# The opening of a two-block model on one core: order of the first loads, one projection alone, rotary angles and turned roots elsewhere, one sum of squares later

## The chip, the cores and the metric

One core of a Trainium2 chip runs the whole program in one launch. The metric is the device time of an execution in microseconds (us). The kernel before takes 2652.35 us (median of three runs, 2652.09 to 2652.76).

## The reference, cut to what matters

Everything is float32. 512 tokens of width 1024 go through a first block of two layers and then a second block (attention, short convolution, a mixture of 32 experts). The change lies in the first block. One layer of it, in short:

```python
y = rms_norm(h, mix_norm[i])                       # root of the mean square over 1024
proj = y @ w_in[i]
x_lru, g_lru, q, k, v, g_ret, u_sgu, v_sgu, g_sgu = jnp.split(proj, split_points, axis=-1)
lru_out = rg_lru(causal_depthwise_conv(x_lru, ...), w_a, b_a, w_x, b_x, lru_lambda[i])   # recurrence
ret_out = retention(q, k, v, positions, ret_norm[i])   # q, k turned by cos/sin(positions * inv)
sgu_out = spatial_gating(u_sgu, v_sgu, ...)
mixed = concat(lru_out * silu(g_lru), ret_out * silu(g_ret), sgu_out * silu(g_sgu))
h = h + mixed @ w_out[i]
z = rms_norm(h, ple_norm[i])
h = h + sigmoid(z @ w_ple_gate[i]) * (p[i] @ w_ple_proj[i])
```

Inside `rg_lru`: `log_a = -8 r softplus(-lambda)`, `a = exp(log_a)`, `u = sqrt(1 - a^2) (i x)` and a scan over the tokens.

## The kernel before, in words

Features lie on the partitions and the 512 tokens on the columns: `hT` is x transposed, eight tiles of 128 x 512. A program of its own runs on each engine, written out in order; semaphores are the only ties between them.

**Weights** come as pieces of 128 x 1024 (512 KB), in the order of `LAYER`: `xl0 xl1 xl2 gl0 xl3 xl4 xl5 gl1..gl5`, then `lru0.*`, `v0.0..v0.3`, `gr0 gr1`, `lru1.*`, `v1.*`, `gr2..gr5`, and q, k, vs, gs, u, wo, g. SyncE (SP) loads them into five raw places (`A_RAW`); a place is free when the piece in it has been split, or, for the unsplit `lru` pieces, used. ScalarE (ACT) makes the high part (a rounded copy, L1786, L1805) and GpSimd (POOL) the low part (L2316), into four places (`A_SPLIT`). `ahead(name)` on ACT splits every piece up to four behind `name`, each as soon as the last use of the place is past. So piece `v0.3` is split by `ahead("gl5")`.

**A product** takes three matmuls per tile of the reduction (high x high, high x low, low x high), so a projection (`project`, 128 outputs) has 24 matmuls of 512 columns. The rows (`ys`) are x times the gain, as a high part (ACT, `gained_high`, L1779) and a low part (VectorE, DVE, `gained_low`, L2037). The norm's factor is not in them: results are multiplied by 1/root (`rn`) when they are read. `side_by_side` runs three projections through the row tiles together, so that it starts with the first tile; it wants all three pieces split first.

**The root**: ACT squares the tiles (L1768), DVE adds them (L2044), TensorE (PE) sums over the partitions with a matrix of ones (`norm_sum`), ACT takes the root (L1773), DVE inverts it (`norm_inverse`, L2053). In layer 0 the sum stands at tile 7 of `side_by_side`, in layer 1 at tile 3, and there it waits for `sq_added`, the whole sum over eight tiles.

**PSUM** has eight banks, in two rings of four: V (gates and others) and A. A group in a ring waits until the one four before it has been read. `gl0..gl5` are V's first six, so `gl4` waits for `gl0`, and `gl5` for `gl1`. DVE scales a gate (L2076), ACT takes its tanh (L1820), and DVE multiplies (`silu2`, L2082), which frees the bank.

**DVE's order after the inverse**: `conv(0..2)`, small work, `scale_gate("gl0")`, `conv(3..5)` with small work between (L2095, L2097, L2100), then in layer 0 `prep_angles` (20 instructions with L1994 first and L2011 last, cosine and sine angles together), then the gates `gl1..gl5`, then the recurrence: decay rates (L2124), three ratios with a reciprocal each (L2130 to L2134), three times the scan (L2140 to L2147), the gates `gr0`, `gr1`.

**ACT's order there**: gates and `ahead`s; `prep_sin` (layer 0, L1744, L1745); tanh of `r` and `i` (L1842, L1844); `ahead("gl5")`; three times Exp and Tanh for DVE's ratios (L1850, L1851); the copy of the turned root `rT` (L1853), whose drain frees its bank (L1854), for which the matmuls of `v0.3` wait; `ahead("v0.3")`; the copies of `v0` (L1858); three square roots (L1862); `gr0`, `gr1`. The second half of the recurrence (g = 1) starts on ACT when `lru_done` has come to 3, and PE's group `r5` waits for ACT's tanh of `r3`.

**Loads at the start**: SP issues piece 0, x0, piece 1, x1, piece 2, x2..x7, pieces 3 and 4. ACT issues `par`, `par2` and the positions (one row spread over 128 partitions), all three on one semaphore, and ACT and DVE wait for all three (48) before their first work.

Of the kernel before, what the change touches and what calls it, by code (L numbers as in the profile page):

```python
# [209 lines left out]
def build(nc, io):  # L210
    ctx = ExitStack()
    with ctx:
# [166 lines left out]
        A = Groups(nc, ctx, "a", [4, 5, 6, 7], a_order, pre=1)  # L379
# [16 lines left out]
        par_in = sem("parameters_in")  # L396
# [1057 lines left out]
        @block.sync  # L1454
        def _(sp):
            for n in range(A_RAW):
                if n < 3:
                    sp.dma_start(pieces[:, n, :], io["pieces"][n]).then_inc(p_in[n], 16)
                for kt in range(n, n + 1) if n < 2 else range(2, DK) if n == 2 else ():
                    sp.dma_start(hT[:, kt, :], io["xT"][kt * P:(kt + 1) * P, :]).then_inc(x_in[kt], 16)  # L1460
                if n >= 3:
                    sp.dma_start(pieces[:, n, :], io["pieces"][n]).then_inc(p_in[n], 16)
# [21 lines left out]
        def _(pe):  # L1484
# [13 lines left out]
            def norm_sum(layer, g, n):  # L1498

                pe.wait_ge(sq_added, n)  # L1500
                pe.wait_ge(A.free, A.reusable(layer, g) if layer >= 0 else 1)
                mm(ps[:, A.bank(g), :], ones[:], sq_sum, True, True).then_inc(A.full, 1)

            for layer in range(L):
# [22 lines left out]
                def side_by_side(pool, names, first, sums):  # L1527


                    ws = [wps[:, L_AT[g] % A_SPLIT].rearrange("p c (k n) -> p c k n", k=DK) for g in names]  # L1530
                    for g in names:
                        high_of(L_AT[g])
                        low_of(L_AT[g])
                        if layer == 0 and L_AT[g] == 1:
                            pe.wait_ge(first_low, 1)
                        pe.wait_ge(pool.free, pool.reusable(layer, g))
                    for k in range(DK):
                        at_ = layer * 2 * DK + first + k + 1
                        pe.wait_ge(yh_ready, at_)
                        for g, w in zip(names, ws):  # L1540
                            mm(ps[:, pool.bank(g), :], w[:, 0, k, :], ys[:, 0, k, :], k == 0, False)
                            mm(ps[:, pool.bank(g), :], w[:, 1, k, :], ys[:, 0, k, :], False, False)
                        sums(k)
                        pe.wait_ge(y_ready, at_)
                        for g, w in zip(names, ws):
                            m = mm(ps[:, pool.bank(g), :], w[:, 0, k, :], ys[:, 1, k, :], False, k == DK - 1)
                            if k == DK - 1:
                                m.then_inc(pool.full, 1)
# [178 lines left out]
        def _(act):  # L1727
            act.dma_start(par_all[:], io["par"]).then_inc(par_in, 16)
            act.dma_start(par2[:], io["par2"]).then_inc(par_in, 16)
            act.dma_start(tmp[:, 2, :].bitcast(I32), io["positions"].partition_broadcast(P)).then_inc(par_in, 16)  # L1730
            def prep_exp():
                act.wait_ge(par_in, 48)
# [3 lines left out]
            def prep_log():  # L1736
                act.wait_ge(prep_v, 2)
                nc.scalar.activation(prep_l, prep_w, ACT.Ln).then_inc(prep_a, 1)
# [3 lines left out]
            def prep_sin():  # L1742
                act.wait_ge(prep_v, 3)
                nc.scalar.activation(rcos, tmp[:, 0, :], ACT.Sin)  # L1744
                nc.scalar.activation(rsin, tmp[:, 1, :], ACT.Sin).then_inc(prep_a, 1)  # L1745
                act.drain()
# [35 lines left out]
            act.wait_ge(par_in, 48)  # L1782
            for k in range(DK):
                if k < 3:
                    act.wait_ge(*landed(0, k))
                    nc.scalar.activation(wps[:, k, 0], pieces[:, k, :], ACT.Copy).then_inc(p_high, 1)  # L1786
# [4 lines left out]
            for k in (DK - 2, DK - 1):  # L1791
                square(k, x_in[k], 16, 0, 0)
            act.wait_ge(*landed(0, 3))
            nc.scalar.activation(wps[:, 3, 0], pieces[:, 3, :], ACT.Copy).then_inc(p_high, 1)

            for layer in range(L):
# [16 lines left out]
                norm_root(A, layer - 1, "next")  # L1813
                if layer == 0:
# [19 lines left out]
                if layer == 0:  # L1834
                    prep_sin()

                for g in range(2):
# [9 lines left out]
                    ahead("gl5" if g == 0 else "gr1")  # L1847
# [15 lines left out]
                    if g == 0:  # L1863
                        ahead("gr0")
# [83 lines left out]
        def _(dve):  # L1948
            dve.sem_inc(V.free, len(V.banks))
# [4 lines left out]
            dve.wait_ge(par_in, 48)  # L1954
# [25 lines left out]
            def prep_rate():  # L1980
                dve.wait_ge(prep_a, 3)
                nc.vector.tensor_tensor(prep_c, prep_c, prep_l, ALU.add)
# [9 lines left out]
            def prep_angles():  # L1992
                posi, ang, turn, turni = tmp[:, 2, :], tmp[:, 3, :], mix[:, 6, :], mix[:, 7, :]
# [4 lines left out]
                for out, quarter in ((tmp[:, 0, :], 0.25), (tmp[:, 1, :], 0.0)):  # L1998
                    nc.vector.tensor_scalar(turni.bitcast(I32), ang, 1.0 / (2 * np.pi), quarter, ALU.mult, ALU.add)
                    dve.drain()  # L2000
                    nc.vector.tensor_copy(turn, turni.bitcast(I32))
                    dve.drain()
                    if quarter:
                        nc.vector.tensor_scalar(turn, turn, -quarter, None, ALU.add)
                        dve.drain()
                    nc.vector.scalar_tensor_tensor(out, turn, -TWO_PI[0], ang, ALU.mult, ALU.add)
                    dve.drain()
                    for part in TWO_PI[1:]:
                        nc.vector.scalar_tensor_tensor(out, turn, -part, out, ALU.mult, ALU.add)
                        dve.drain()  # L2010
                    nc.vector.tensor_scalar(out, out, 3.1415925, -3.1415925, ALU.min, ALU.max)  # L2011
                    dve.drain()
                dve.sem_inc(prep_v, 1)
# [41 lines left out]

            for k in range(DK):
                if k == 2:
                    dve.wait_ge(p_high, 2)
                    nc.vector.tensor_tensor(wps[:, 1, 1], pieces[:, 1, :], wps[:, 1, 0].bitcast(F32),
                                            ALU.subtract).then_inc(first_low, 1)  # L2060
                gained_low(k, 0, 0, "mix_norm")
                if k >= 3:
                    add_square(k - 2, 0, 0)
            for k in range(DK - 2, DK):
                add_square(k, 0, 0)

            for layer in range(L):
# [4 lines left out]
                norm_inverse(2 * layer + 1)  # L2072

# [41 lines left out]
                conv(5)  # L2115
                if layer == 0:
                    prep_angles()
                gates([f"gl{i}" for i in range(1, 6)], lambda i: 1 + i, 1)

                for g in range(2):  # L2120
# [5 lines left out]

                    for m in range(3):
# [175 lines left out]
        def _(pool):  # L2303
            def constants_in():
                for dst, name in ((ident[:], "ident"), (tri[:], "tri"), (cst[:], "cst")):
# [18 lines left out]
            for n in range(A_SPLIT):  # L2324
                if n == 1:
# [161 lines left out]
```

## Time and profile before

| what | us |
|---|---|
| median of the runs | 2652.35 |
| profiled execution | 2650.75 |
| its span, first to last instruction | 2648.9 |
| TensorE busy | 2501.9 (94%) |
| VectorE busy | 1896.0 (72%) |
| ScalarE busy | 1326.5 (50%) |
| GpSimd busy | 727.6 (27%) |
| mean granted TensorE clock | 0.974 |

The span is what the trace covers; the profiled execution's own time has 1.85 us more around it. Times in the rows are from the span's start. Layer 0 goes to about 488 us, layer 1 to about 1009 us; the second block fills the rest. A loop's matmuls overlap: one shows 389 ns, but the starts follow each other closer.

### The profile page before, as it was taken

To read this page: it belongs to the slowest core of one execution; us is meant where nothing else is said; L and a number is where in the kernel's file an instruction comes from. 1 tells how busy PE (TensorE), PEld (TensorE's weight loads), DVE (VectorE), ACT (ScalarE), POOL (GpSimd) and SP (SyncE) were. 2 spreads that over 40 slices of the span, in tenths; PEclk is the share of its full clock that TensorE was granted. 3 is DMA by queue.
4 is the path that set the end of the run, shared out by engine and by line. 5 is a ranking of instruction groups with operands and counts; after the bars stand their busy time and mean duration, and the time that the engine had idled before them with its cause. 6 is when DMAs were issued, how large, how long until landed. Compare 5 with 4: busy or idle time off the path is not lost.

```text
span 2648.9 us, 32704 instructions
## 1 busy us (share of the span) xinstructions
PE 2501.9 (94%) x11479; PEld 1987.2 (75%) x11479; DVE 1896.0 (72%) x1732; ACT 1326.5 (50%) x1224; POOL 727.6 (27%) x401
## 2 busy tenths in 40 slices
PE   7799999999999998899886999999999999999995
PEld 6577788676777875687465788888888888888884
DVE  6668541565876053276425999999999999999994
ACT  4342233424313232233423777777777777777772
POOL 4324265342424630034122212222111222111220
PEclk9899999999999999999986999999999999999998
DMA  6223232223323326523005999999999999999993
GB/s 210 87 96 88 64 120 88 72 64 112 104 71 104 96 88 224 191 64 94 3 12 207 369 371 377 366 371 370 366 372 374 366 369 370 367 371 375 368 364 104
DMA packets 104497, 572.57 MB, mean 216 GB/s; under 512 B 14193, under 2 KB 14337, under 8 KB 54353
## 3 DMA queue, kind: packets, MB, share of 16 engines
q1 hardware_dynamic: 93552, 539.27, 54.9%
q0 software_dynamic: 10432, 31.81, 4.8%
q8 instruction: 52, 0.85, 0.1%
q10 hardware_dynamic: 432, 0.40, 0.1%
q14 instruction: 29, 0.23, 0.0%
HBM read 559.37 MB, written 24.12 MB: 220 GB/s over the span
## 4 chain that ended last, share of the span: by engine, by line
PE 86%; DVE 7%; ACT 2%; DVEq 2%; issue 1%; DMA 1%; ACTq 1%; SPq 0%; POOL 0%; POOLq 0%
PE ps L1486 83%; PE ps L1167 2%; DVE scr L2100 1%; DVE y_split L2037 1%; DVEq L2047 1%; PE ps L643 0%; DVE mix L2147 0%; DVE scr L2145 0%; DMA pieces<-in_pieces 0%; DMA scr<-in_positions 0%; ACTq L1854 0%; DMA acc_rows<-rows,lst 0%; DVEq L2275 0%; DVE scr L958 0%; DVE w_split L1294 0%
## 5 line engine op out<-in xcount | busy, mean ns | idle before, releaser
L1294 DVE TENSOR_TENSOR w_split<-raw,w_split 128x2048 fp32r<-128x2048 f32 x386 | 877.5, 2288 | 54.4 <-ACT w_split L1246 43.6
L1486 PE MATMUL ps<-y_split,pieces_split 128*128 128x512 f32 x3600 | 840.0, 394 | 32.8 <-POOL pieces_split L2316 17.7
L1246 ACT ACTIVATE w_split<-raw 128x2048 fp32r<-128x2048 f32 x386 | 735.9, 1916 | 198.1 <-PE ps L1486 178.3
L1486 PEld LDWEIGHTS ps<-y_split,pieces_split 128*128 128x128 f32 x3600 | 677.9, 189 | 183.1 <-issue 40.9
L1486 PE MATMUL ps<-w_split,rows_T 128*128 128x512 f32 x3096 | 753.5, 394 | 1.9 <-DVE rows_T L1300 1.9
L1486 PEld LDWEIGHTS ps<-w_split,rows_T 128*128 128x128 f32 x3096 | 576.5, 189 | 119.8 <-DVE rows_T L1300 2.5
L2316 POOL TENSOR_TENSOR pieces_split<-pieces,pieces_split 128x1024 fp32r<-128x1024 f32 x171 | 416.6, 2444 | 804.4 <-ACT pieces_split L1805 569.1
L1805 ACT ACTIVATE pieces_split<-pieces 128x1024 fp32r<-128x1024 f32 x144 | 151.5, 1058 | 462.6 <-PE ps L1486 425.1
L1486 PE MATMUL ps<-w_split,hidden_T 128*128 128x512 f32 x1536 | 363.2, 392 | 0.1
L1486 PEld LDWEIGHTS ps<-w_split,hidden_T 128*128 128x128 f32 x1536 | 285.7, 188 | 70.7 <-DVE hidden_T L1300 12.2
L1358 POOL COPY rows_i<-slot_tokens 128x1 int32 (+1 forms) x34 | 59.7, 1755 | 408.4 <-PE ps L1167 374.1
L1486 PE MATMUL ps<-scr 128*128 128x512 f32 (+3 forms) x432 | 136.2, 460 | 5.3 <-ACT scr L836 3.6
L1486 PE MATMUL ps<-pieces_split,y_split 128*128 128x512 f32 (+1 forms) x672 | 130.2, 354 | 9.6 <-ACTq L1854 9.6
L1486 PEld LDWEIGHTS ps<-pieces_split,y_split 128*128 128x128 f32 x672 | 109.2, 194 | 27.5 <-ACTq L1854 10.4
L1374 POOL DMA_INDIRECT acc_rows<-rows,lst x33 | 65.3, 1979 | 228.7 <-ACT rows L1255 228.7
L2249 DVE TENSOR_TENSOR hT<-ps,hT 128x512 f32<-128x512 f32 x16 | 11.0, 688 | 155.0 <-PE ps L1486 154.1
L1486 PEld LDWEIGHTS ps<-scr 128*128 128x128 f32 x432 | 74.2, 190 | 61.4 <-issue 45.5
L2022 DVE RECIPROCAL scr<-scr 128x512 f32<-128x512 f32 (+1 forms) x24 | 75.7, 3153 | 45.3 <-ACT scr L1761 41.4
L1360 POOL DMA_INDIRECT rows<-h_rows,rows_i x34 | 93.2, 2742 | 29.6 <-issue 29.6
L1365 POOL COPY lst<-slot_tokens 128x1 int32 (+1 forms) x34 | 9.1, 268 | 310.6 <-DMA acc_rows<-rows,lst 302.7
L1486 PE MATMUL ps<-pieces,cond 128*2 128x128 f32 x768 | 87.7, 276 | 0.8 <-issue 0.8
L1486 PEld LDWEIGHTS ps<-pieces,cond 128*2 128x2 f32 x768 | 65.2, 86 | 22.5 <-issue 3.1
(250 smaller groups left out, 2072.7 us busy)
## 6 DMA issues: line engine op xcount, KB each, us to landing
raw<-in_w_moe SPq DMA_DIRECT2D x386, 1024.0 KB, 7.3
pieces<-in_pieces SPq DMA_DIRECT2D x229, 512.0 KB, 3.7
scr<-in_ple SPq DMA_DIRECT2D x2, 1536.0 KB, 6.9
acc_rows<-in_zeros POOLq DMA_DIRECT2D x5, 512.0 KB, 11.3
hT<-in_xT SPq DMA_DIRECT2D x8, 256.0 KB, 8.2
h_rows<-scr SPq DMA_DIRECT2D x4, 512.0 KB, 3.2
mix<-acc_rows SPq DMA_DIRECT2D x4, 512.0 KB, 5.4
out_T<-hT SPq DMA_DIRECT2D x8, 256.0 KB, 2.1
```

Of the source, the lines that this page charges most:

```text
L1167: m = pe.transpose(ps[:, bank, j * P:(j + 1) * P], src[:, j * P:(j + 1) * P], ident[:])
L1246: nc.scalar.activation(wsp[:, p % SPLIT, 0], raw[:, p % RAW, :], ACT.Copy).then_inc(high, 3 if p == 1 else 1)
L1294: nc.vector.tensor_tensor(wsp[:, p % SPLIT, 1], raw[:, p % RAW, :], wsp[:, p % SPLIT, 0].bitcast(F32), ALU.subtract).then_inc(low, 3 if p ...
L1358: nc.gpsimd.tensor_copy(rows_i[:, s:s + 1], list_tok[:, bass.ds(b, 1)])
L1360: nc.gpsimd.indirect_dma_start(out=xg[:, s, :], out_offset=None, in_=h2_dram[:, :], in_offset=bass.IndirectOffsetOnAxis(ap=rows_i[:, s:s + ...
L1374: nc.gpsimd.indirect_dma_start(out=acc_dram[:, :], out_offset=bass.IndirectOffsetOnAxis(ap=lst[:, s, 0:1].bitcast(U32), axis=0), in_=y_sb[ ...
L1486: return pe.matmul(out, lhsT, rhs, start=start, stop=stop)
L1805: nc.scalar.activation(wps[:, n % A_SPLIT, 0], pieces[:, place_of(after, at_), :], ACT.Copy).then_inc(p_high, 1)
L2022: nc.vector.reciprocal(r, r)
L2037: nc.vector.scalar_tensor_tensor(ys[:, 1, k, :], hT[:, k, :], par_all[:, layer_, at_:at_ + 1], ys[:, 0, k, :].bitcast(F32), ALU.mult, ALU. ...
L2047: dve.drain()
L2316: nc.gpsimd.tensor_tensor(wps[:, n % A_SPLIT, 1], pieces[:, place_of(layer, at_), :], wps[:, n % A_SPLIT, 0].bitcast(F32), ALU.subtract).t ...
```

## The change

```diff
# SP: loads at the start
-                if n < 3:
-                    sp.dma_start(pieces[:, n, :], ...).then_inc(p_in[n], 16)
-                for kt in range(n, n + 1) if n < 2 else range(2, DK) if n == 2 else ():
+                sp.dma_start(pieces[:, n, :], ...).then_inc(p_in[n], 16)
+                for kt in range(DK) if n == 0 else ():
                     sp.dma_start(hT[:, kt, :], ...).then_inc(x_in[kt], 16)
# PE
                 def opening_sum(k):
-                    if k == (DK - 1 if layer == 0 else 3):
+                    if layer and k == DK - 1:
                         norm_sum(layer - 1, "next", 2 * layer + 1)
-                side_by_side(A, ("xl0", "xl1", "xl2"), 0, opening_sum)
-                for name, _, pool, g in LAYER[3:12]:
+                first = ("xl0", "xl1", "xl2") if layer else ("xl0",)
+                side_by_side(A, first, 0, opening_sum)
+                for name, _, pool, g in LAYER[len(first):12]:
+                    if layer == 0 and name == "gl0":
+                        pe.wait_ge(sq_added, 1)
+                        mm(ps[:, V.bank("gl3"), :], ones[:], sq_sum, True, True).then_inc(first_sum, 1)
                     project(pools[pool], g)
# ACT
-            act.dma_start(par2[:], io["par2"]).then_inc(par_in, 16)
-            act.dma_start(tmp[:, 2, :].bitcast(I32), io["positions"].partition_broadcast(P)).then_inc(par_in, 16)
+            act.dma_start(par2[:], io["par2"]).then_inc(par2_in, 16)
-            act.wait_ge(par_in, 48)
+            act.wait_ge(warm, 1)
+            nc.scalar.activation(small[:, 1:2], small[:, 0:1], ACT.Copy)
+            act.wait_ge(par_in, 16)
+            first_high(0)
             for k in range(DK):
-                if k < 3: (wait for piece k, its high part)
                 act.wait_ge(x_in[k], 16)
                 gained_high(k, 0, "mix_norm")
-                if k >= 2:
-                    square(k - 2, x_in[k - 2], 16, 0, 0)
-            (square 6, square 7, high part of piece 3)
+            first_high(1)
+            square(0, x_in[0], 16, 0, 0)
+            square(1, x_in[1], 16, 0, 0)
+            first_high(2)
+            for k in range(2, DK):
+                square(k, x_in[k], 16, 0, 0)
+                if k == 3:
+                    first_high(3)
...
-                if layer == 0:
-                    prep_sin()                       # ahead of the recurrence
...
-                    ahead("gl5" if g == 0 else "gr1")
+                    if g == 0:
+                        nc.scalar.activation(rT, full(A, "rt")[:, 0:8], ACT.Copy)
+                        act.drain().then_inc(A.free, 1)
+                    else:
+                        ahead("gr1")
                     for m in range(3): (Exp and Tanh for the ratios)
-                    if g == 0:
-                        nc.scalar.activation(rT, full(A, "rt")[:, 0:8], ACT.Copy)
-                        act.drain().then_inc(A.free, 1)
                     ahead("v0.3" if g == 0 else "v1.1")
                     ... (copies of v, square roots)
                     if g == 0:
+                        if layer == 0:
+                            prep_sin()
                         ahead("gr0")
# DVE
+            nc.vector.memset(small[:, 0:2], 0.0).then_inc(warm, 1)
-            dve.sem_inc(V.free, len(V.banks))
+            dve.sem_inc(V.free, len(V.banks) - 1)    # the fourth after norm_inverse in layer 0
-            dve.wait_ge(par_in, 48)
+            dve.wait_ge(par_in, 16)
             (low part of piece 0 in place of piece 1, ahead of the eight gained_low;
              the seven add_square after all eight gained_low, no longer between them)
                 conv(5)
-                if layer == 0:
-                    prep_angles()
                 gates([f"gl{i}" for i in range(1, 6)], lambda i: 1 + i, 1)
+                if layer == 0:
+                    prep_positions()                 # positions to float, times inv_freq
+                    prep_angles(rcos, 0.25)
                 for g in range(2):
                     for m in range(3): (decay rates, L2124)
+                    if layer == 0 and g == 0:
+                        prep_angles(rsin, 0.0)
+                        dve.sem_inc(prep_v, 1)
# POOL
             def constants_in():
+                pool.dma_start(std[:, 1, :].bitcast(I32), io["positions"].partition_broadcast(P)).then_inc(positions_in, 16)
...
-                if n == 1:
+                if n == 0:
                     pool.wait_ge(first_low, 1)       # DVE makes this piece's low part
```

The ring A also loses the count of one that layer 0's sum of squares took at its head (`pre=1`), since that sum is now in a bank of V.

## Rows read from the trace of the kernel before

**Rows 1.** The page: busy us, share of the span and instructions of each engine.

```profile
PE 2501.9 (94%) x11479; PEld 1987.2 (75%) x11479; DVE 1896.0 (72%) x1732; ACT 1326.5 (50%) x1224; POOL 727.6 (27%) x401
```

**Rows 2.** Chain that ended last, 0 to 200 us: start, us, what.

```profile
1.67 7.00 DMA scr<-in_positions
...
14.72 2.67 POOL pieces_split L2316
...
80.24 0.43 DVE scr L1994
...
88.94 0.43 DVE scr L2011
```

**Rows 3.** Timeline, 0 to 45 us: start, us, engine, line, operation [idle before <-releaser].

```profile
13.31 1.21 DVE L2059 TENSOR_TENSOR pieces_split<-pieces,pieces_split 128x1024 fp32r<-128x1024 f32 x1
...
17.74 17.24 PE L1486 MATMUL ps<-y_split,pieces_split 128*128 128x512 f32 x69 [17.74 <-POOL pieces_split L2316]
...
23.64 2.24 DVE L2044 TENSOR_TENSOR scr<-scr 128x512 f32<-128x512 f32 x3
...
34.82 1.02 PE L1486 MATMUL ps<-scr,ones 128*128 128x512 f32 x2
```

**Rows 4.** Line 1460 (loads of x tiles): durations ns, first and last start us.

```profile
L1460 SPq DMA_DIRECT2D hT<-in_xT x8: 422/440/532, 1.2 to 5.6; - x8
...
DMA to landing us min/median/max: 4.3/8.2/8.9
```

**Rows 5.** Timeline, 36 to 90 us, DVE: the first convolution, its first instruction, a later one.

```profile
40.01 0.69 DVE L2095 TENSOR_TENSOR scr<-ps,scr 128x512 f32<-128x512 f32 x1
...
41.95 8.34 DVE L2100 SCALAR_TENSOR_TENSOR scr<-scr,par_all 128x512 f32<-128x512 f32 x3
...
51.81 2.40 DVE L2100 SCALAR_TENSOR_TENSOR scr<-scr,par_all 128x512 f32<-128x512 f32 x3
```

**Rows 6.** Timeline of PE alone, 35 to 130 us.

```profile
35.27 44.78 PE L1486 MATMUL ps<-y_split,pieces_split 128*128 128x512 f32 x195
91.68 7.60 PE L1486 MATMUL ps<-y_split,pieces_split 128*128 128x512 f32 x24 [11.63 <-DVE mix L2082]
99.12 12.18 PE L1486 MATMUL ps<-scr,pieces 128*128 128x512 f32 x28
```

**Rows 7.** Stretches, PE alone: length, busy (matmuls), granted clock, DMA share, GB/s.

```profile
17.74:19.74 2.00, 2.00 (x5) 1.00 1.03 367
...
91.68:93.68 2.00, 2.00 (x5) 0.50 0.00 0
```

**Rows 8.** Timeline, 86 to 165 us: around the recurrence's first half.

```profile
115.13 1.06 ACT L1805 ACTIVATE pieces_split<-pieces 128x1024 fp32r<-128x1024 f32 x1 [3.11 <-DMA pieces<-in_pieces]
...
119.44 20.94 PE L1486 MATMUL ps<-pieces_split,y_split 128*128 128x512 f32 x84 [4.84 <-ACTq L1854]
...
145.75 0.69 DVE L2143 SCALAR_TENSOR_TENSOR mix<-scr,mix 128x512 f32<-128x512 f32 x1 [11.36 <-ACT mix L1862]
...
160.60 3.70 PE L1486 MATMUL ps<-scr,pieces 128*128 128x512 f32 x8 [0.77 <-ACT mix L1842]
```

**Rows 9.** Timelines of layer 1's opening: all engines, and PE alone.

```profile
523.96 0.75 DVE L2037 SCALAR_TENSOR_TENSOR y_split<-hT,par_all,y_split 128x512 fp32r<-128x512 f32 x1
...
525.39 2.07 PE L1486 MATMUL ps<-scr,ones 128*128 128x512 f32 x2 [5.48 <-DVEq L2047]
...
536.80 0.69 DVE L2095 TENSOR_TENSOR scr<-ps,scr 128x512 f32<-128x512 f32 x1 [5.29 <-PE ps L1486]
...
576.42 0.69 DVE L2082 SCALAR_TENSOR_TENSOR mix<-mix,ps 128x512 f32<-128x512 f32 x1
...
586.02 12.18 PE L1486 MATMUL ps<-scr,pieces 128*128 128x512 f32 x28
...
606.22 21.61 PE L1486 MATMUL ps<-pieces_split,y_split 128*128 128x512 f32 x84 [4.73 <-ACTq L1854]
```

**Rows 10.** Timeline of PE alone, 130 to 1150 us: a short wait.

```profile
316.09 1.98 PE L1486 MATMUL ps<-scr,ones 128*128 128x512 f32 x4 [1.72 <-ACT scr L1893]
```

More of the change, by code:

```diff
@@ L395, in build @@
         x_in = [sem(f"x_in{k}") for k in range(DK)]
-        par_in = sem("parameters_in")
+        par_in, par2_in, positions_in = sem("parameters_in"), sem("parameters2_in"), sem("positions_in")
+        warm = sem("small_cleared")
+        first_sum = sem("first_norm_sum")
         p_in = [sem(f"piece_in{i}") for i in range(A_RAW)]
@@ L1500, in norm_sum @@
                 pe.wait_ge(sq_added, n)
-                pe.wait_ge(A.free, A.reusable(layer, g) if layer >= 0 else 1)
+                pe.wait_ge(A.free, A.reusable(layer, g))
                 mm(ps[:, A.bank(g), :], ones[:], sq_sum, True, True).then_inc(A.full, 1)
@@ L1533, in side_by_side @@
                         low_of(L_AT[g])
-                        if layer == 0 and L_AT[g] == 1:
-                            pe.wait_ge(first_low, 1)
                         pe.wait_ge(pool.free, pool.reusable(layer, g))
@@ L1743, in prep_sin @@
                 act.wait_ge(prep_v, 3)
-                nc.scalar.activation(rcos, tmp[:, 0, :], ACT.Sin)
-                nc.scalar.activation(rsin, tmp[:, 1, :], ACT.Sin).then_inc(prep_a, 1)
-                act.drain()
+                nc.scalar.activation(rcos, rcos, ACT.Sin)
+                nc.scalar.activation(rsin, rsin, ACT.Sin).then_inc(prep_a, 1)
             def squares(first, n, tile, ready, ready_at, buf, cols=S, free_at=0, rd=None, fr=None):
@@ L1811, in full @@
                     return ps[:, pool.bank(g), :]
-                norm_root(A, layer - 1, "next")
-                if layer == 0:
+                if layer:
+                    norm_root(A, layer - 1, "next")
+                else:
+                    act.wait_ge(first_sum, 1)
+                    nc.scalar.activation(rn, ps[:, V.bank("gl3"), :], ACT.Sqrt, bias=EPSC, scale=1.0 / D)
+                    act.drain().then_inc(root_ready, 1)
                     prep_exp()
@@ L1846, in _ @@
                         act.drain().then_inc(ri_ready, 1)
-                    ahead("gl5" if g == 0 else "gr1")
+                    if g == 0:
+                        nc.scalar.activation(rT, full(A, "rt")[:, 0:8], ACT.Copy)
+                        act.drain().then_inc(A.free, 1)
+                    else:
+                        ahead("gr1")
                     for m in range(3):
@@ L1990, in prep_rate, with prep_positions @@
                 dve.drain()
-            def prep_angles():
-                posi, ang, turn, turni = tmp[:, 2, :], tmp[:, 3, :], mix[:, 6, :], mix[:, 7, :]
+            posi, ang, turn, turni = std[:, 1, :], std[:, 0, :], sq[:, 0, :], sq[:, 1, :]
+            def prep_positions():
+                dve.wait_ge(positions_in, 16)
                 nc.vector.tensor_copy(ang, posi.bitcast(I32))
@@ L1997, in prep_angles @@
                 dve.drain()
-                for out, quarter in ((tmp[:, 0, :], 0.25), (tmp[:, 1, :], 0.0)):
-                    nc.vector.tensor_scalar(turni.bitcast(I32), ang, 1.0 / (2 * np.pi), quarter, ALU.mult, ALU.add)
+            def prep_angles(out, quarter):
+                nc.vector.tensor_scalar(turni.bitcast(I32), ang, 1.0 / (2 * np.pi), quarter, ALU.mult, ALU.add)
+                dve.drain()
+                nc.vector.tensor_copy(turn, turni.bitcast(I32))
+                dve.drain()
+                if quarter:
+                    nc.vector.tensor_scalar(turn, turn, -quarter, None, ALU.add)
                     dve.drain()
-                    nc.vector.tensor_copy(turn, turni.bitcast(I32))
+                nc.vector.scalar_tensor_tensor(out, turn, -TWO_PI[0], ang, ALU.mult, ALU.add)
+                dve.drain()
+                for part in TWO_PI[1:]:
+                    nc.vector.scalar_tensor_tensor(out, turn, -part, out, ALU.mult, ALU.add)
                     dve.drain()
[L2003 to L2013, printed above, removed]
+                nc.vector.tensor_scalar(out, out, 3.1415925, -3.1415925, ALU.min, ALU.max)
+                dve.drain()
             def p_(name, i, n=1):
@@ L2054, in norm_inverse @@
                 dve.drain().then_inc(r_ready, 1)
+            dve.wait_ge(p_high, 1)
+            nc.vector.tensor_tensor(wps[:, 0, 1], pieces[:, 0, :], wps[:, 0, 0].bitcast(F32),
+                                    ALU.subtract).then_inc(first_low, 1)
             for k in range(DK):
[L2057 to L2060, printed above, removed]
                 gained_low(k, 0, 0, "mix_norm")
-                if k >= 3:
-                    add_square(k - 2, 0, 0)
-            for k in range(DK - 2, DK):
+            for k in range(1, DK):
                 add_square(k, 0, 0)
@@ L2115, in _ @@
                 conv(5)
+                gates([f"gl{i}" for i in range(1, 6)], lambda i: 1 + i, 1)
                 if layer == 0:
-                    prep_angles()
-                gates([f"gl{i}" for i in range(1, 6)], lambda i: 1 + i, 1)
+                    prep_positions()
+                    prep_angles(rcos, 0.25)
                 for g in range(2):
```

19 lines of the change are left out of this document (8 added, 11 removed).

## The prediction

> **What bounds the kernel now.** I read the page's shares first: TensorE (PE) is busy 94% of the span, so a change pays only where it removes an idle stretch of PE or a stretch at PE's lower clock [rows 1]. Then PE's own timeline of the first block, for the stretches where it stands still: 17.74 us before its first matmul [rows 3]; 11.63 us before `gl5` [rows 6]; 4.84 us inside `v0` in layer 0, 4.73 at the same place in layer 1, and 5.48 at layer 1's sum of squares [rows 8, 9]. The chain of waits says who makes them: in the opening the positions' load (1.67 to 8.67) and the last low part of three pieces (to 17.39); later DVE's angle work, from 80.24 to 89.37 [rows 2]. Last, the clock: PE's first stretches show 5 matmuls in 2.00 us both at the start and after the 11.63 us wait, where the granted clock is 0.50, the lower of its two levels (1.2 GHz) [rows 7]. The sum is made on the profiled execution (2650.75 us, its span 2648.9 plus 1.85 around it) and taken off the median of the runs, 2652.35, which stands 1.6 higher.
>
> PE's pace at the upper level is 44.78 / 195 = 0.230 us a matmul, 5.51 a projection of 24 [rows 6].
>
> **Term 1, the opening (8.2 us).** What counts is when PE makes the norm's sum, now at 34.82 [rows 3], since DVE's chain of convolutions hangs on it: conv(0) starts 5.2 later, at 40.01 [rows 5].
> The eight x tiles are issued from 1.2 to 5.6 and take up to 8.9 us [rows 4], so the last lands near 14.5. Ahead of it stand three pieces, eight tiles and the positions (4.0 MB with the parameters); after the change one piece and eight tiles (2.75 MB). At the 367 GB/s of [rows 7] the 1.3 MB less are 3.5 us: x7 near 11, piece 1 near 12.5. Without the positions ACT can begin near 5; 1.06 for piece 0's high part [rows 8] and 1.21 for its low part on DVE [rows 3] let PE start near 7.5. From there `xl0` is paced by DVE's low parts, eight at 0.75 [rows 9], to 13.5, and the last of them may stand behind POOL's low part of piece 1 (2.67 [rows 2]): `xl0` ends near 15.5. `xl1` and `xl2` follow at 5.51 each: 26.5, and the sum at 26.6. The squares have to be in by then: ACT has piece 1, two squares and piece 2 done near 15, and of DVE's seven adds (2.24 for three [rows 3]) I let three stand behind a POOL operation of 2.67: about 25.3. PE sets it, with 1.3 to spare. That is 34.82 - 26.6 = 8.2. PE's slow first matmuls lie in the paced stretch and cost nothing there. Bounds: no sooner than the squares, 25.3 (9.5 saved); no later than with all transfers where they were, x7 at 14.5, high part of piece 1 at 16.5, three projections less the part beside, 29.5 (5.3 saved).
>
> The low parts bear on a rule of the Trainium skill. `conv(0)`'s three operations on two SBUF inputs take 8.34 us beside POOL's low parts, the same three later 2.40 [rows 5]. "SBUF — State Buffer", section "SBUF: two separate sides", says that a DVE operation with two SBUF inputs and a GpSimd one take a shared port pair in turn, each whole. By that rule the seven adds, now after the eight low parts and so beside POOL's pieces 2 and 3, are held three times, as counted above; without it the squares are in near 20 and the sum does not move, since PE sets it.
>
> Small edits with one answer: the empty copy on ACT at the start (a table load in time that ACT waits anyway), one load less issued by ACT, the same 13 issues on SP in another order, one issue more on POOL ahead of the constants. Cost 0, hidden under the wait for the first bytes; if not, one issue, under 0.6 us. The positions are wanted only near 81, some 50 us after their issue.
>
> **Term 2, the angles (9.1 us).** From the sum on, DVE's and POOL's order to the end of conv(5) is unchanged, so it moves as a block by 8.2. `gl5` waits for `gl1`'s product on DVE, which stood behind the angles. They go: 80.24 to 89.37 is 9.1 [rows 2]. The wait of 11.63 [rows 6] becomes 2.5: PE is again ahead of conv(5), and what is late next is conv(5) itself. `gl5` starts at 91.68 - 8.2 - 9.1 = 74.4.
> Where they go: the cosine half (5.3) after `gl5`'s product, 81 to 87, while PE does `r` and `i` for 12.2 us [rows 6] from 79.9; the third rate is asked for near 93. The sine half (3.8) stands between the rates and the ratios, where DVE would wait for ACT's Exp and Tanh. Behind it are the ratios and the scan; DVE there has 11.36 us of idle time before the roots come [rows 8]. Off it go 4.84 and 1.65 (term 4) and 3.8: 1.1 stays even if nothing else came sooner, so the angles cost 0. If the cover is gone they cost up to 3.8. `prep_sin` on ACT (two table loads, two operations, about 4) moves behind the square roots, under DVE's 12 us of scans; 0, with up to 2 if `gr2`'s low part, then later on POOL, meets another scan operation, and a gain of as much if it meets none.
>
> **Term 3, the clock at `gl5` (1.9 us).** `gl5` takes 99.12 - 91.68 = 7.44 [rows 6], at the lower level; with a wait of 2.5 I take 5.51. After the 1.72 us wait of [rows 10] two sums take 1.98, the price of [rows 3] (1.02 for one), so the clock had not fallen; after 4.84 it had. 2.5 is nearer to 1.72. Bounds 0 to 1.9.
>
> **Term 4, the turned root sooner, twice (6.5 and 7.1 us).** The copy of `rT` stood behind `v0.3`'s split, which waited 3.11 for its load [rows 8], and behind six operations for the ratios. Now it is next after the last tanh, before PE has done the first 12 matmuls of `v0`. The waits of 4.84 and 4.73 go, and with them the slow matmuls after: 20.94 - 84 x 0.230 = 1.65, and 21.61 - 19.3 = 2.3 [rows 8, 9]. The split of `v0.3`, now later, is wanted 16 us after `v0` starts and is there after 9. What follows (`v0` copies, roots, scans, `r5`) hangs on the end of `v0` and moves with it, the 0.77 us wait with it [rows 8].
> Layer 0: 8.2 + 9.1 + 1.9 + 4.8 + 1.7 = 25.7.
>
> **Term 5, layer 1's sum at tile 7 (7.5 us).** PE stood from 519.91 to 525.39 with tiles 4 to 7 undone. The last row part is ready at 524.7 [rows 9]. Now PE does tile after tile: with the ready times it comes to the sum near 527.6 and ends the three projections near 528.7, against 537.2: 8.4 sooner. But the sum is 2.2 later, so DVE's chain starts at 527.6 + 5.2 = 532.8, where it started at 536.80 because PE was late [rows 9]: 4.0 sooner. `gl1`'s product, done at 577.1, comes at 573.1; PE, 528.7 + 8 x 5.51, would like `gl5` at 572.8. So `gl5` starts at 573.1, against 586.02 - 5.51 = 580.5: 7.4, and a new wait of 0.3. Bounds: 4 (if DVE's chain were to bind all the way) to 8.4.
> Layer 1: 7.5 + 7.1 = 14.6. The rest of the program has no tie to an absolute time and moves whole.
>
> Sum: 25.7 + 14.6 = 40.3, so 2652.35 - 40.3 = **2612.0 us**.
>
> **Rivals.**
> (a) *The opening gives less*: transfers or the squares hold the sum back to 29.5 or more, and the clock falls at `gl5` as well. For: the x tiles' landing is worked out, not seen. Against: even then 5.3 stays. 2612 + 2.9 + 1.9 = 2617, up to 2621 with a scan operation held.
> (b) *The turned root brings nothing*: `v0` waits as long for something else, its pieces for instance, as ACT did for a load of 3.11 [rows 8]. Against: pieces `v0.0` to `v0.2` were split long before. 2612 + 13.6 = 2625.6.
> (c) *Slower than before: the clock does not rise.* `xl0` alone has three matmuls per 0.75 us of DVE, 0.69 of work, so PE starts with a small gap in each tile. If it then stays at the lower level, a projection costs 24 x 0.4 = 9.6 [rows 7], 4.1 more. From 10 projections on this eats the 40.3; over the twelve and `v0` (four more) it is 66, and the time 2678. Against: the projections behind `xl0` are gapless, and after each wait the rows show the clock back within a single projection.
> The Trainium skill has this as a case: "TensorE: Matmul & The Clock Gate", section "A second HAM failure mode: psum-queue depth-cycling", says that small idle gaps between groups of matmuls can make the clock go up and down. The paced `xl0` is such a pattern for 8 tiles; nothing behind it is.
> (d) *Given back*: something downstream that does not move takes up most of it, within 0.2% of before. I find no such row.
>
> **Chances.** The forecast's case (2607 to 2617) 0.66; better than it, with the sum at the squares' bound and no scan operation held (2603 to 2607) 0.07; (a) 0.15; (b) 0.06; (c) 0.03; (d) 0.03. Range: 2604 to 2621. A difference under 0.2% (5.3 us) can't be told from none. Faster by over 0.2%: 0.94; within: 0.03; slower: 0.03.
>
> **What would show it.** First matmul near 7.5, the norm's sum near 26.6 and conv(0) near 31.8 (term 1); no angle work between conv(5) and the gates, a wait of about 2.5 before `gl5` near 74.4 (term 2) and full pace behind it (term 3); no wait inside `v0` in either layer, 96 matmuls in about 22 us (term 4); in layer 1 no wait at the sum, `gl5` 7.4 sooner relative to the layer's start (term 5). Wrong if the sum comes behind 30, if DVE's ratios end after ACT's copies of `v0`, or if a wait of over 3 us stands before `gl5`.

## The result and the profile after

The changed kernel takes 2612.06 us (median of four runs, 2611.15 to 2612.63) against 2652.31 for the one before (2652.09 to 2652.76): a ratio of 0.9848, 95% interval 0.9831 to 0.9865, so 40.2 us faster. The forecast was 2612.0. A second set of five runs gave 2611.17. (In `u_root` and `u_open` below one run was disturbed, 10130 and 3255 us; the medians given leave it out.) The profiled execution took 2611.84, its span is 2610.0; that is 38.9 under the profiled execution of the kernel before, since the part behind layer 1's `v0`, which the change does not touch, took 1.3 us longer in it (2022.5 for 2021.2).

The page's line of busy times, beside [rows 1]: the work is the same, PE's idle time went from 147 to 113.5 us and its busy time fell by the slow matmuls that became fast.

```profile
PE 2496.5 (96%) x11479; PEld 1985.1 (76%) x11479; DVE 1895.9 (73%) x1733; ACT 1326.9 (51%) x1224; POOL 737.4 (28%) x402
```

The chain of waits, 0 to 200 us (start, us, what), in place of [rows 2]: neither positions nor angles stand in it. The parameters' load, piece 0 and then PE itself lead to the norm's inverse.

```profile
0.73 4.10 DMA par_all<-in_par
4.86 1.06 ACT pieces_split L1785
5.95 1.23 DVE pieces_split L2074
7.34 20.02 PE ps L1485 x74
28.04 3.35 DVE scr L2070
...
73.98 19.34 PE ps L1485 x52
```

The load of the x tiles (time to landing, beside [rows 4]), the same bytes behind less:

```profile
L1461 SPq DMA_DIRECT2D hT<-in_xT x8: 422/432/522, 1.2 to 4.5; - x8
...
DMA to landing us min/median/max: 4.3/5.5/6.2
```

Four marks are used from here on: the first matmul; "the sum", the two matmuls of layer 0's norm sum; `r`, the start of the 28 matmuls of `r` and `i`; and the end of `v0`, which is the start of the 48 matmuls behind its 96.

The timeline of PE alone, layer 0, beside [rows 3, 6, 8], and after the dots layer 1, beside [rows 9]. The waits of 11.63, 4.84, 0.77, 5.48 and 4.73 us are gone; one of 3.10 stands before `gl5`.

```profile
7.34 19.15 PE L1485 MATMUL ps<-y_split,pieces_split 128*128 128x512 f32 x72 [7.34 <-POOLq L2350]
26.33 1.02 PE L1485 MATMUL ps<-scr,ones 128*128 128x512 f32 x2
26.79 44.10 PE L1485 MATMUL ps<-y_split,pieces_split 128*128 128x512 f32 x192
73.98 7.32 PE L1485 MATMUL ps<-y_split,pieces_split 128*128 128x512 f32 x24 [3.10 <-DVE mix L2099]
81.14 12.18 PE L1485 MATMUL ps<-scr,pieces 128*128 128x512 f32 x28
...
93.59 22.07 PE L1485 MATMUL ps<-pieces_split,y_split 128*128 128x512 f32 x96
115.50 11.04 PE L1485 MATMUL ps<-y_split,pieces_split 128*128 128x512 f32 x48
...
138.39 12.08 PE L1485 MATMUL ps<-pieces_split,y_split 128*128 128x256 f32 x96
...
486.57 16.22 PE L1485 MATMUL ps<-y_split,pieces_split 128*128 128x512 f32 x69
502.63 1.02 PE L1485 MATMUL ps<-scr,ones 128*128 128x512 f32 x2
503.09 50.22 PE L1485 MATMUL ps<-y_split,pieces_split 128*128 128x512 f32 x219
553.14 12.18 PE L1485 MATMUL ps<-scr,pieces 128*128 128x512 f32 x28
...
565.59 22.07 PE L1485 MATMUL ps<-pieces_split,y_split 128*128 128x512 f32 x96
587.49 11.04 PE L1485 MATMUL ps<-y_split,pieces_split 128*128 128x512 f32 x48
```

The same marks in the kernel before, on the same view: layer 1's first rows at 511.86, its `r` and `i` at 586.02, the first gates behind its `v0` at 627.66. So the change is 40.17 us ahead at the end of `v0` in layer 1 (627.66 - 587.49), of which 25.29 come from layer 0.

### The profile page after: what moved, and what is told of

Same layout as the page of the kernel before. It is cut to its first block, busy times and chain, and to the rows that moved or that the text cites. A ratio compares the mean times of both kernels' runs of the same rounds, so it can differ in the third digit from the quotient of the medians.

```text
span 2610.0 us, 32704 instructions
## 1 busy us (share of the span) xinstructions
PE 2496.5 (96%) x11479; PEld 1985.1 (76%) x11479; DVE 1895.9 (73%) x1733; ACT 1326.9 (51%) x1224; POOL 737.4 (28%) x402
## 4 chain that ended last, share of the span: by engine, by line
PE 88%; DVE 6%; ACT 2%; issue 1%; DVEq 1%; DMA 1%; ACTq 0%; SPq 0%; POOLq 0%
PE ps L1485 85%; PE ps L1169 2%; DVE scr L2117 1%; DVE y_split L2054 0%; DVEq L2064 0%; PE ps L645 0%; DVE mix L2168 0%; DVE scr L2166 0%; DMA acc_rows<-rows,lst 0%; PE ps L1421 0%; DVE w_split L1296 0%; DVE scr L960 0%; PE ps L681 0%; DMA mix<-acc_rows 0%; DVE hT L2270 0%
## 5 line engine op out<-in xcount | busy, mean ns | idle before, releaser
L1485 PEld LDWEIGHTS ps<-scr 128*128 128x128 f32 x432 | 74.2, 190 | 61.4 <-issue 45.5
L1367 POOL COPY lst<-slot_tokens 128x1 int32 (+1 forms) x34 | 15.5, 455 | 313.4 <-DMA acc_rows<-rows,lst 304.1
```

Source lines behind the costliest of these rows:

```text
L1367: nc.gpsimd.tensor_copy(lst[:, s, 0:1], list_tok[:, bass.ds(b, 1)])
L1485: return pe.matmul(out, lhsT, rhs, start=start, stop=stop)
```

## The experiments

Each is the changed kernel with at most one thing changed, except `both` with two, so "moves" are against its trace. The median of the changed kernel is 2612.1 in one set and 2611.2 in another, and that of the kernel before lies between 2652.3 and 2653.2. The part behind layer 1's `v0`, which only `tail_sum` and `both` touch, took from 2019.9 to 2024.5 us in the other ten profiled executions. Differences of under 2 us are therefore read from the trace, at a mark inside the first block, and not from the total.

**u_root**, term 4 undone:

```diff
-                    if g == 0: (copy of rT, drain, A.free)
-                    else: ahead("gr1")
+                    ahead("gl5" if g == 0 else "gr1")
                     for m in range(3): (Exp and Tanh)
+                    if g == 0: (copy of rT, drain, A.free)
```

> The changed kernel with only the turned root put back behind v0.3's split and the six operations for the ratios, in both layers. Theory (the root's place is worth 4.84 + 1.65 us in layer 0 and 4.73 + 2.3 us in layer 1, wait and lower clock behind it): a wait of 4.7 to 4.9 inside v0 returns in both layers, the 96 matmuls of v0 take 28.6 and 29.2 us in place of 22.07, and the time is 2612.1 + 13.5 = 2625.6. Rival (v0's end is not on the path, the recurrence on VectorE is): the wait returns but r5 moves by less, since VectorE's 5.93 us of idle time before the roots takes it up; +8 or less.

2625.3 us, 13.3 slower. PE's timeline shows both waits again, and the end of layer 1's `v0` at 600.41 for 587.49: 12.9 later, half of it in each layer. VectorE's idle time did not take it up: the theory stands, in the trace 0.6 under its 13.5.

```profile
101.21 20.92 PE L1485 MATMUL ps<-pieces_split,y_split 128*128 128x512 f32 x84 [4.69 <-ACTq L1864]
...
579.86 20.71 PE L1485 MATMUL ps<-pieces_split,y_split 128*128 128x512 f32 x84 [4.79 <-ACTq L1864]
```

**u_sum**, term 5 undone:

```diff
-                    if layer and k == DK - 1:
+                    if layer and k == 3:
```

> The changed kernel with only layer 1's sum of squares back at tile 3. Theory: the 5.48 us wait returns at the sum, PE ends the three projections 8.4 later, and gl5 (or the recurrence's r) starts 7.5 later relative to the layer's start: 2612.1 + 7.5 = 2619.6. Rival 1 (VectorE's chain of convolutions binds layer 1): it starts only 4.0 later, so +4 (2616). Rival 2 (PE alone binds and the clock's fall is the rest): +8.4 (2620.5).

2619.3 us, 7.3 slower. From layer 1's first rows to `r` it takes 561.08 - 486.26 = 74.8 us, against 66.6: the whole loss lies there.

```profile
486.26 8.05 PE L1485 MATMUL ps<-y_split,pieces_split 128*128 128x512 f32 x33
499.80 2.07 PE L1485 MATMUL ps<-scr,ones 128*128 128x512 f32 x2 [5.49 <-DVEq L2064]
500.89 60.35 PE L1485 MATMUL ps<-y_split,pieces_split 128*128 128x512 f32 x255
561.08 12.18 PE L1485 MATMUL ps<-scr,pieces 128*128 128x512 f32 x28
```

8.2 by this trace, 7.6 by that of the kernel before (586.02 - 511.86 = 74.2): above the theory's 7.5, and near PE's own 8.4 of the second rival, so VectorE's chain binds hardly or not at all. The two figures differ by the slow matmuls behind the wait: eight of them follow each other at 0.43 us in `u_sum`, four in the kernel before. `sum6` asks that directly.

**sum6**, the sum one tile sooner:

```diff
-                    if layer and k == DK - 1:
+                    if layer and k == 6:
```

> The changed kernel with layer 1's sum of squares at tile 6 in place of 7. The squares are added up at 500.1 us of the changed kernel's trace and PE comes to tile 6's place near 500.5: no wait, the sum 2.1 sooner, and with it VectorE's convolutions. Theory (in layer 1 of the changed kernel PE binds, VectorE's chain has some slack at gl5): no change, 2612.1 within 1. Rival (VectorE's chain binds in layer 1): 2610 or below, recurrence's r 2 us sooner relative to the layer's start.

The sum comes without a wait and 2 us sooner, and `r` starts 552.19 - 485.61 = 66.58 us after the layer's first rows, where the changed kernel takes 66.57. PE alone binds there. The median, 2610.3, is 1.8 lower than the first set of the changed kernel and 0.9 lower than the second, and that is not layer 1.

```profile
499.63 1.02 PE L1485 MATMUL ps<-scr,ones 128*128 128x512 f32 x2
500.09 52.26 PE L1485 MATMUL ps<-y_split,pieces_split 128*128 128x512 f32 x228
552.19 12.18 PE L1485 MATMUL ps<-scr,pieces 128*128 128x512 f32 x28
```

**u_angles**, term 2 undone:

```diff
                 conv(5)
+                if layer == 0: (positions, both halves of the angles)
                 gates([f"gl{i}" for i in range(1, 6)], ...)
-                if layer == 0: (positions, cosine half)
...
-                    if layer == 0 and g == 0: (sine half)
```

> The changed kernel with both halves of the angle work back between conv(5) and the gates, prep_sin left behind the square roots. Theory: gl5 waits 3.1 + 9.1 = 12.2 us and starts near 83.1; the clock has fallen behind 3.1 us already, so nothing more is lost there (7.16 against 7.44 for gl5): 2612.1 + 9.1 + 0.3 = 2621.5. Rival 1 (part of it is given back, since the angles no longer stand beside the recurrence, so that VectorE's ratios end sooner): +7 or less. Rival 2 (a longer wait costs more clock): +11.

2620.5 us, 8.5 slower, `r` at 90.17 for 81.14: 9.0. The sum came 0.5 sooner in this execution, so from the sum to `r` it is 9.5: 9.2 of wait and 0.3 of slow matmuls. The gates shift by the angle work and nothing of it comes back from the recurrence: at the end of layer 1's `v0` it is still 9.0.

```profile
82.72 7.62 PE L1485 MATMUL ps<-y_split,pieces_split 128*128 128x512 f32 x24 [12.34 <-DVE mix L2099]
90.17 12.18 PE L1485 MATMUL ps<-scr,pieces 128*128 128x512 f32 x28
```

**u_open**, term 1 undone (loads in the old order, positions on ScalarE and waited for, three projections side by side with the sum at tile 7, squares between the tiles):

```diff
-                first = ("xl0", "xl1", "xl2") if layer else ("xl0",)
+                first = ("xl0", "xl1", "xl2")
...
+            act.dma_start(std[:, 1, :]..., io["positions"]...).then_inc(positions_in, 16)
+            act.wait_ge(positions_in, 16)      # and on VectorE
```

> The changed kernel with only the opening undone: old order of the loads, positions loaded by ScalarE and waited for, three projections side by side with the sum at tile 7, squares between the row tiles. Theory: first matmul at 17.7, sum at 34.8, everything behind it as a block 8.4 later, the wait before gl5 the same 3.1: 2612.1 + 8.4 = 2620.5. Rival (the wait of 3.1 at gl5 is the opening's doing, and with the old one PE and VectorE come together): the wait shrinks and the loss is 5.5 or less.

2619.6 us, 7.5 slower; in the trace `r` is at 91.06, 9.9 later.

```profile
18.47 18.41 PE L1488 MATMUL ps<-y_split,pieces_split 128*128 128x512 f32 x69 [18.47 <-POOL pieces_split L2347]
36.72 1.02 PE L1488 MATMUL ps<-scr,ones 128*128 128x512 f32 x2
37.18 44.78 PE L1488 MATMUL ps<-y_split,pieces_split 128*128 128x512 f32 x195
83.92 7.30 PE L1488 MATMUL ps<-y_split,pieces_split 128*128 128x512 f32 x24 [1.96 <-DVE mix L2109]
```

The sum is later than in the kernel before (34.82), by 0.7 for the first matmul and by 1.2 for slower matmuls behind it. The wait before `gl5` is 1.96 and not 3.10, for which the rival had another reason: three of the 195 matmuls here follow the sum inside the three projections (0.69 us), which in the changed kernel all lie ahead of it. PE so comes to `gl5` that much later after the sum, while VectorE starts from the sum in both. The other 0.45 lies on VectorE: in the changed kernel its third convolution has a gap of 0.52 us in which it waits for nothing that the trace shows, and here (and in `pos_act`, whose wait is 2.68) that gap is missing. Total and trace disagree by 2 us, as much as the untouched part varies (2020.6 here, 2022.5 in the changed kernel).

**pos_act**, one half of term 1:

```diff
+            act.dma_start(std[:, 1, :]..., io["positions"]...).then_inc(positions_in, 16)
+            act.wait_ge(positions_in, 16)      # and on VectorE
-                pool.dma_start(std[:, 1, :]..., io["positions"]...).then_inc(positions_in, 16)
```

> The changed kernel with the positions loaded by ScalarE as its third load and waited for by ScalarE and VectorE before their first work, all else as changed. It splits term 1: Theory (the opening's gain is mostly that nothing waits for the positions): the positions land near 9.3 as in the kernel with the opening undone, first matmul near 11.9 in place of 7.3, x7 about 1 us later, the norm's sum 3.3 to 4.5 later (near 30), and the rest as a block: 2612.1 + 3.9 = 2616. Rival (it is the order of the loads and xl0 alone, the positions only fill time in which x is awaited): sum later by under 1.5.

2615.0 us, 3.0 slower; first matmul at 11.48, the sum at 29.32 (3.0 later), `r` at 84.97 (3.8 later). The first matmul is 4.1 later but the sum only 3.0, because this execution began with six slow matmuls (0.43 us apart) and the changed kernel's with twelve, 1.2 us of difference. So the positions are 3 to 4 us of the opening's 8.5. The rest, 4.5 to 5.5, is the order of the loads with the single projection, taken together; the two were not tried apart.

**gl1_sooner**, the 3.10 us wait taken away:

```diff
                 conv(4)
+                scale_gate("gl1", 1)
                 if layer == 0: (prep_rate)
+                silu2("gl1", 1, 1)
                 conv(5)
-                gates([f"gl{i}" for i in range(1, 6)], lambda i: 1 + i, 1)
+                gates([f"gl{i}" for i in range(2, 6)], lambda i: 2 + i, 2)
```

> The changed kernel, gl1's gate (scaling and product) moved ahead of conv(5) on VectorE, in both layers. Theory (the 3.1 us wait before gl5 and the low clock behind it, 7.16 for 24 matmuls in place of 5.5, are all that is left there): gl1's product is done near 69.3, ahead of PE's 70.9, so both go: 2612.1 - 3.1 - 1.65 = 2607.3, and nothing in layer 1, where PE does not wait there. Rival (the next wait takes it over: the third bank, or r5's wait for the recurrence): -2 or less, with a new wait in v0 or before r5.

2604.3 us, 7.7 faster than the changed kernel. From the sum to `r` it takes 75.02 - 25.18 = 49.84, against 54.81: 5.0, near the theory's 4.75. The other 2.7 stand at no mark that the edit reaches. In the profiled execution the untouched part was the shortest of all, 2019.9, and the sum 1.15 sooner; and `both` below is 4.3 under `tail_sum` alone. So 5 is the edit's share, and that the rest is chance is likely but not shown. No new wait comes in its place, and `gl1` to `gl5` run at the upper clock.

```profile
25.18 1.02 PE L1485 MATMUL ps<-scr,ones 128*128 128x512 f32 x2
25.64 49.54 PE L1485 MATMUL ps<-y_split,pieces_split 128*128 128x512 f32 x216
75.02 12.18 PE L1485 MATMUL ps<-scr,pieces 128*128 128x512 f32 x28
```

**tail_sum**, term 5's step where layer 1 ends:

```diff
-                if layer == L - 1:
-                    norm_sum(layer, "next", 2 * layer + 3)
...
                 modulation(j)
+                if j == 0:
+                    norm_sum(L - 1, "next", 2 * L + 1)
+                    pe.wait_ge(V.free, L * V.n + len(V.banks))
```

(PE's waits for free banks ahead of the modulations move with it, each to the first use of its bank.)

> The changed kernel with term 5's step taken a third time: at the end of layer 1 the sum of squares, for which PE waits 7.09 us, goes behind the first quarter-row of modulation matmuls (modulation 0, 64 matmuls, 7.15 us, that need no norm). Theory: the wait goes, the sum is made 1.1 later at the upper clock, and modulation 1 starts about 10 us sooner (near 967.5 in place of 977.7); PE binds to the sums of the second block, so 2612.1 - 10 = 2602. Rival (the norm's chain, root, inverse, eight products, is the path there): the time stays or rises by 1.1, and the gain turns into a longer wait at the sums of the squares behind modulation 5.

2601.5 us, 10.6 faster. Modulation 1 starts at 967.07; its transposes come at 975.06 for 984.62, so it and the modulations behind it are 9.0 us sooner, once the 0.5 us that this trace was ahead before is taken off. That is 1 under the theory's 10; 0.74 us of it is a new wait for a weight load. The norm's chain is not the path there. The changed kernel first, then this run:

```profile
966.44 2.07 PE L1485 MATMUL ps<-scr,ones 128*128 128x512 f32 x2 [7.09 <-DVEq L2064]
969.28 15.42 PE L1485 MATMUL ps<-pieces,cond 128*2 128x128 f32 x128 [0.77 <-issue]
```

```profile
958.85 7.15 PE L1490 MATMUL ps<-pieces,cond 128*2 128x128 f32 x64
966.02 1.12 PE L1490 MATMUL ps<-scr,ones 128*128 128x512 f32 x2
967.07 5.40 PE L1490 MATMUL ps<-pieces,cond 128*2 128x128 f32 x48
973.22 1.91 PE L1490 MATMUL ps<-pieces,cond 128*2 128x128 f32 x16 [0.74 <-DMA pieces<-in_pieces]
```

**after_again**, the changed kernel once more, unchanged:

> The changed kernel itself once more, as a control: what differs between executions of one program. Theory (the clock's low stretch at the start and the part behind layer 1 vary by 1 to 2 us each, whatever the kernel): the median within 2 us of 2612.1, the sum in layer 0 between 24.9 and 26.4, the recurrence's r between 80.1 and 81.2, the part behind layer 1's v0 2020 to 2024 us. Rival (each kernel has its own fixed time there): the trace repeats 26.33, 81.14 and 2022.5 within 0.2.

2611.2 us; the sum at 25.98, `r` at 80.69, the untouched part 2022.1. All of the theory's numbers held, but two executions of this one program are only 0.3 to 0.5 apart at each mark, less than its 1 to 2 us, and too few to tell its cause. Over the seven other programs with this opening the sum comes from 24.97 to 26.24, which is why a mark in layer 0 is good to about 1 us and not better.

**both**, `gl1_sooner` and `tail_sum` together:

> The changed kernel with gl1's gate ahead of conv(5) and the last sum behind modulation 0, the two steps that each moved PE sooner alone. Theory (they stand on different stretches and add): 5.0 in layer 0 and 9.1 at the end of layer 1, 2612.1 - 14.1 = 2598, or 2596 by the medians of the two alone. Rival (one of the medians was luck of the untouched part): 2600 or more.

2597.1 us (2595.7 to 2598.7), ratio to the kernel before 0.9791 (0.9777 to 0.9804): 14 to 15 us faster than the changed kernel and the best version tried.

## Why the prediction was right, and where it was not

*Term 1, the opening: 8.2 forecast, 8.5 measured* (34.82 to 26.33). First matmul 7.34 (7.5), last x tile in by 10.7 (11), the sum 26.33 (26.6), set by PE. `u_open` gives 9.9 at `r`, `pos_act` 3 to 4 for the positions' share. One step inside it failed and its number came out by luck. I had `xl0` paced by VectorE's low parts to 15.5, with PE's slow first matmuls at no cost beneath. But the low parts were done at 12.47, POOL held none of them, and PE never waited for one: its first twelve matmuls start 0.43 us apart and the rest 0.23, without a gap, and `xl1` starts at 15.44. So the slow matmuls set this stretch and are paid in full: with six of them, in `gl1_sooner`, `xl1` starts at 14.29 and the sum is 1.15 sooner.

The seven adds of the squares bear on the shared port pair. Three, begun at 14.19, 16.83 and 18.98, took 1.89, 2.05 and 2.71 us and end 0.55 after a low part on POOL each; the other four, with no POOL work on two SBUF inputs beside them, took 0.69. The last ends at 24.8 (25.3), and the sum did not wait for it. The rule of "SBUF — State Buffer", section "SBUF: two separate sides", of the Trainium skill, by which three were counted as held, agrees.

*Term 2, the angles: 9.1 forecast, 9.0 measured* by `u_angles` at `r`, and 9.2 from the sum to `gl5` (47.65 for 56.86 in the kernel before). The wait left was put at 2.5 and is 3.10; what was missed are the three matmuls that in the old order follow the sum (0.69 us), as the rows of `u_open` show. The sine half beside the recurrence cost nothing: VectorE still has 5.93 us of idle time before the roots.

```profile
121.05 0.69 DVE L2164 SCALAR_TENSOR_TENSOR mix<-scr,mix 128x512 f32<-128x512 f32 x1 [5.93 <-ACT mix L1873]
```

*Term 3, the clock at `gl5`: 1.9 forecast, 0.3 measured.* This step failed. I had "2.5 is nearer to 1.72" from [rows 10] and so took the upper clock; `gl5` took 7.16 us in place of 7.44. The stretches (length, busy, granted clock, ...) show it, the changed kernel first, then `u_open` behind 1.96 us, then the kernel before behind 1.72 us:

```profile
73.98:75.98 2.00, 2.00 (x5) 0.56 0.00 0
```

```profile
83.92:85.92 2.00, 2.00 (x7) 0.81 0.00 0
85.92:87.92 2.00, 2.00 (x6) 0.50 0.00 0
```

```profile
316.09:318.09 2.00, 2.00 (x5) 1.00 0.00 0
318.09:320.09 2.00, 2.00 (x10) 1.00 0.60 119
```

After 1.96 us of waiting the granted clock was at the lower level (1.2 GHz) for a stretch, after 1.72 us it was not. The step that failed is the choice by the nearer row: a wait can't be priced by its length alone (the last section shows a fall behind still shorter waits), and both ends had to stay open, as the bound of 0 to 1.9 did. `gl1_sooner` shows the term's size: wait and low clock together were worth 5.0.

*Term 4, the turned root: 6.5 + 7.1 forecast.* `v0` takes 22.07 us in both layers, with no wait; from `r` to `v0`'s end the changed kernel needs 34.36 (115.50 - 81.14) for 41.09 (140.21 - 99.12), so 6.7, and in layer 1 34.35 for 41.64, so 7.3. `u_root` gives 6.5 and 6.5. The gain has two parts of different nature, the wait (4.8) and the slow matmuls behind it, and only the first is the same in each execution.

*Behind `v0` in layer 0*, 0.6 us more was gained than forecast: the 0.77 us wait before `r5` went. Of VectorE's three products after the scans (L2168) the one held by POOL took 2.61, as before one took 2.90 at another place; that is 0.3 of it, and a gap of 0.43 between the scans in the kernel before, gone in the changed one, is the rest. I had put this at 0, between -2 and +2.

*Term 5, layer 1's sum: 7.5 forecast, 7.6 measured* (74.16 to 66.57 from the layer's first rows to `r`). The size is right and its reason half wrong: I had VectorE's chain bind at `gl5` with a wait of 0.3. There is no wait there, and `sum6` shows that the sum could be 2 us sooner without any effect. The two halves of the working did not fit: with PE done with the three projections at 537.2, `gl5` would have come at 537.2 + 8 x 5.51 = 581.3 and not at the 580.5 taken from the row. Counted back from 580.5, PE was done at 536.4, its own gain was 7.7 and not 8.4, and no wait was left for VectorE to make.

At the end of `v0` in layer 1 the forecast was 40.3 us and the trace shows 40.2: the 1.6 lost at term 3 came back in pieces, 0.3 in term 1, 0.2 + 0.2 in term 4, 0.6 behind it, 0.1 in term 5. So the hit on the total is in part luck: it is better than its parts. The four undone parts add up to 12.9 + 7.9 + 9.0 + 9.9 = 39.7 at that mark.

*Rivals.* (a) did not happen on the side of the loads, but its second half, the fallen clock, did. (b) is out by `u_root`. (c), the clock that stays low behind the paced projection, did not happen: the stretches of 2 us from 7.34 on hold 5, 7, 7, then 10 or more matmuls. It was not tested either, since `xl0` was not paced. The pattern of small idle gaps that the Trainium skill describes ("TensorE: Matmul & The Clock Gate", section "A second HAM failure mode: psum-queue depth-cycling") did not arise in it, so no run here shows what such gaps would do. (d): nothing was given back within the first block.

## What to carry to other kernels

An instruction that waits for a whole sum should stand in its engine's order where the sum is ready, and not where its operands begin: that was worth 7.6 us in layer 1 and another 9 at the end of it. A tiny copy that frees a bank goes ahead of the long work on its engine, and small work that others don't wait for goes where its engine waits anyway. A wait on TensorE costs itself and, in some cases, slow matmuls behind it; price both, and leave the second open, since the wait's length alone does not decide it.

## What the runs showed of the hardware that I had not expected

- The wait's length decides neither whether the granted clock falls nor what the fall costs. In the midst of dense matmuls a wait of 1.96 us had a fall behind it and one of 1.72 had none. But in the second block of `pos_act` the clock fell behind waits of 1.30 and 1.03 us with a few short transposes between them (granted 0.74 and then 0.50), while in the changed kernel the same waits left it at 1.00. `tail_sum` and `both` show a fall at that place too. The changed kernel first, then `pos_act`:

```profile
1273.07 0.88 PE L645 MATMUL ps<-ident,scr 128*128 128x128 f32 x6 [1.03 <-DVE scr L960]
1274.84 5.42 PE L1485 MATMUL ps<-scr 128*128 128x512 f32 x12 [0.90 <-ACT scr L838]
```

```profile
1277.92 1.54 PE L645 MATMUL ps<-ident,scr 128*128 128x128 f32 x6 [1.03 <-DVE scr L960]
1280.36 7.31 PE L1485 MATMUL ps<-scr 128*128 128x512 f32 x12 [0.90 <-ACT scr L838]
```

- The price of a fall before `gl5`. From the end of the wait to `r` it takes 7.14 us behind a wait of 1.96, 8.42 behind 2.68, 7.16 and 8.24 behind 3.10 and 3.11 (the changed kernel and `u_sum`), and 7.45 behind 12.34, for the same 24 matmuls: the price does not follow the wait's length. It follows how many of them are slow: behind 2.68 twelve start 0.43 us apart, behind 1.96 and 3.10 seven.

```profile
76.55 8.57 PE L1485 MATMUL ps<-y_split,pieces_split 128*128 128x512 f32 x24 [2.68 <-DVE mix L2102]
84.97 12.18 PE L1485 MATMUL ps<-scr,pieces 128*128 128x512 f32 x28
```

- The opening's 72 matmuls took from 17.95 to 19.19 us in programs in which they are the same, and the part behind layer 1's `v0` from 2019.9 to 2024.5. The first lies in the slow matmuls at the start, six or twelve of them. Much of the second is the clock as well: in the three shortest parts (2019.9 to 2020.4) it was at the lower level for 96 us, in the other seven for 102 to 109, and 2.6 us of `pos_act`'s 2024.5 is the fall shown above (1277.92 to 1288.45, for 1273.07 to 1281.04).
